# A two-layer decoder trunk in float32: chunk order of the opening, and the last matmuls and root of the end

## The chip, the cores and the metric

The kernel runs on one core of one Trainium2 chip. The time is that of one execution on the device, in microseconds; the median of several runs counts.

## The reference

Two layers over 256 tokens of width 1024, all in float32. Each layer is: x plus half a SwiGLU feed-forward (width 2816) of the normalised x, then x plus a token mixer, then x plus half another SwiGLU. The mixer of layer 0 pools and convolves, that of layer 1 is a gated spatial unit. A last RMSNorm ends it.

```python
def rms_norm(x, g):
    y = x * lax.rsqrt(jnp.mean(x * x, axis=-1, keepdims=True) + EPS)
    return y * g
def swiglu_ffn(x, w_in, w_out):
    gate, up = jnp.split(x @ w_in, 2, axis=-1)
    return (jax.nn.silu(gate) * up) @ w_out
...
for i in range(DEPTH):
    x = x + 0.5 * swiglu_ffn(rms_norm(x, ffn1_norm[i]), ffn1_w_in[i], ffn1_w_out[i])
    x = x + (pool_conv_mixer if i % 2 == 0 else sgu_mixer)(rms_norm(x, mix_norm[i]), ...)
    x = x + 0.5 * swiglu_ffn(rms_norm(x, ffn2_norm[i]), ffn2_w_in[i], ffn2_w_out[i])
return rms_norm(x, final_norm)
```

## The kernel before

The 256 tokens are two tiles of 128 (t = 0, 1). Every float32 operand is kept as a high part (`w_hi`, `xn_hi`, `act_hi`) and a low part (`w_lo`, `xn_lo`, `act_lo`), and `three` makes a product of three matmuls: high x high, high x low, low x high. Weights come in slabs of 128 x 2048 (1 MB), 154 of the feed-forwards and mixers in the order of use. SP loads a slab into one of three `raw` buffers, ScalarE copies it to `w_hi` (ring of six), VectorE subtracts and writes `w_lo` (`lo_split` counts finished slabs). The load of slab n waits until slab n-3 has been split by VectorE. Each engine has its order written out by hand, and semaphores tie them together.

A feed-forward takes units of 256 hidden columns: one slab holds gate and up columns side by side for the first four 128-row chunks of the 1024 inputs, the next slab for the last four. For each token tile the eight chunks accumulate in one bank (`ga` for tile 0, `ub` for tile 1), 512 columns wide. ScalarE takes the Silu of the gate half (`gate_rows`), VectorE multiplies (`product_rows`, which frees the bank) and block-transposes (`to_blocks`); small transfers finish the transpose, and `step_out` multiplies with a slab of `w_out` into four accumulators `acc[t][h]` (token tile t, column half h).

The opening (first unit, slabs 0 and 1, then 2 and 3) is special. The input x arrives in four quarters (`load_x(t, h)`), slabs 0 and 1 in four transfers each (`load_quarters`): a landed pair of chunks counts in `early_landed[n]`, the second pair in `raw_landed[n]`. TensorE transposes x (`first_pairs(t)` the first half of tile t in pairs of chunks, `transposes(0, t, (1,))` the second half), ScalarE writes high parts (`pair_hi`, `second_hi`), VectorE low parts (`pair_lo`, `second_lo`). The norm's root isn't applied to x but later, in `gate_rows` and `product_rows`. `piece` splits part of a slab: `hi_piece` and `lo_piece` count the parts. `opening_unit` runs, by `chunk_rows`, chunks 0 to 3 of tile 0 (with the transposes of tile 1 ahead of chunk 2 and those of tile 0's second half ahead of chunk 3), chunks 0 to 3 of tile 1, then 4 to 7 of tile 0, then 4 to 7 of tile 1. Before it stand warm-up matmuls on constants, some of which wait for the first high parts, low parts and piece.

At the end `slab_out` of the last slab adds both 128-row parts to `acc[1][0]` and `acc[1][1]`, part by part; `half_out` tells VectorE that the left half is complete, `slab_used` the right one. `final(1)` then adds to the residual, multiplies by the last gain, ScalarE squares and sums each half (`ms`), VectorE adds the two sums and EPS (`ms_eps`), GpSimd takes the root (`root`, a power of -0.5), VectorE scales the left half and ScalarE the right half, and SP stores both.

## Time and profile before

| | us |
|---|---|
| median of 3 runs | 893.14 (893.04 to 893.53) |
| the profiled execution | 892.8 |
| its span, first to last instruction | 891.1 |
| TensorE busy in the span | 883.0 (99%) |
| VectorE busy | 566.5 (64%) |
| ScalarE busy | 420.8 (47%) |
| GpSimd busy | 55.6 (6%) |
| mean granted clock of TensorE | 0.998 |

The span leaves out 1.7 us around the instructions. In the page L followed by a number is a line of the kernel, PE is TensorE, PEld its weight loads, DVE VectorE, ACT ScalarE, POOL GpSimd, SP the queue that issues the loads and stores. `w_hi`, `xn_hi` and so on are the program's names for buffers. A busy TensorE includes the time that a matmul spends in the pipeline: a wide matmul (128x512) is shown with 0.39 us.

### The profile page before, as it was taken

How to read it: one execution, taken by the hardware profiler on the slowest of the kernel's cores; microseconds unless marked ns; L12 is line 12 of the kernel's file. 1: busy time of each engine (PE TensorE's matmuls, PEld its weight loads, DVE VectorE, ACT ScalarE, POOL GpSimd, SP SyncE). 2: the span in 40 equal slices, each digit the busy share in tenths (PEclk: the TensorE clock that was granted, in tenths of full speed). 3: DMA queues.
4: the chain of work that ended last, by engine and by line, in shares of the span. 5: the costliest groups of instructions: out<-in, count | busy, mean ns of one | idle time of the engine just before them, and what ended most of it. 6: DMA issues, size and time to landing. Idle time of an engine off the chain costs nothing.

```text
span 891.1 us, 11345 instructions
## 1 busy us (share of the span) xinstructions
PE 883.0 (99%) x4130; PEld 739.0 (83%) x4130; DVE 566.5 (64%) x595; ACT 420.8 (47%) x470; POOL 55.6 (6%) x60
## 2 busy tenths in 40 slices
PE   9999999999999999999999999999999999999997
PEld 8888888889888888888888888888899888888885
DVE  5865565578967756556477556555778666656643
ACT  7644443358744635345345444343663445434432
POOL 1000000406710000000000000000010000000000
PEclk9999999999999999999999999999999999999999
DMA  8987566545254975776639756746575368675721
GB/s 285 294 271 241 178 220 236 177 142 192 70 188 129 300 233 178 243 239 218 208 99 298 258 183 216 240 164 189 168 283 164 120 192 273 216 239 165 240 90 48
DMA packets 149933, 180.18 MB, mean 202 GB/s; under 512 B 7885, under 2 KB 134377, under 8 KB 149896
## 3 DMA queue, kind: packets, MB, share of 16 engines
q1 hardware_dynamic: 149880, 179.67, 61.7%
q8 instruction: 24, 0.39, 0.2%
q14 instruction: 13, 0.11, 0.0%
q10 hardware_dynamic: 16, 0.00, 0.0%
HBM read 168.11 MB, written 1.05 MB: 190 GB/s over the span
## 4 chain that ended last, share of the span: by engine, by line
PE 96%; issue 1%; POOL 1%; ACT 1%; DVE 0%; POOLq 0%; ACTq 0%
PE ga L1246 10%; PE ub L1246 10%; PE ga L1248 10%; PE ub L1248 10%; PE ga L1247 10%; PE ub L1247 10%; PE acc L1246 10%; PE acc L1248 10%; PE acc L1247 10%; PE tp L1308 1%; PE ga L1432 1%; POOL w_lo L509 1%; PE ga L1521 0%; PE tp L1614 0%; DVE w_lo L858 0%
## 5 line engine op out<-in xcount | busy, mean ns | idle before, releaser
L858 DVE TENSOR_TENSOR w_lo<-raw,w_hi 128x2048 fp32r<-128x2048 f32 x147 | 333.4, 2291 | 75.0 <-ACT w_hi L549 73.0
L549 ACT ACTIVATE w_hi<-raw 128x2048 fp32r<-128x2048 f32 x151 | 284.2, 1907 | 21.8 <-DMA raw<-in_ffn_w_in_dram 12.7
L1246 PE MATMUL acc<-w_hi,act_hi 128*128 128x512 f32 x416 | 163.8, 394 | 0.0
L1248 PE MATMUL acc<-w_hi,act_lo 128*128 128x512 f32 x416 | 162.0, 390 | 0.0
L1247 PE MATMUL acc<-w_lo,act_hi 128*128 128x512 f32 x416 | 161.9, 389 | 0.0
L1246 PE MATMUL ga<-w_hi,xn_hi 128*128 128x512 f32 x384 | 150.7, 393 | 0.0
L1246 PE MATMUL ub<-w_hi,xn_hi 128*128 128x512 f32 x384 | 149.5, 389 | 0.0
L1248 PE MATMUL ga<-w_hi,xn_lo 128*128 128x512 f32 x384 | 149.5, 389 | 0.0
L1247 PE MATMUL ga<-w_lo,xn_hi 128*128 128x512 f32 x384 | 149.5, 389 | 0.0
L1248 PE MATMUL ub<-w_hi,xn_lo 128*128 128x512 f32 x384 | 149.5, 389 | 0.0
L1247 PE MATMUL ub<-w_lo,xn_hi 128*128 128x512 f32 x384 | 149.4, 389 | 0.0
L1248 PEld LDWEIGHTS acc<-w_hi,act_lo 128*128 128x128 f32 x416 | 78.1, 188 | 16.5
L1247 PEld LDWEIGHTS acc<-w_lo,act_hi 128*128 128x128 f32 x416 | 78.2, 188 | 15.6
L1246 PEld LDWEIGHTS acc<-w_hi,act_hi 128*128 128x128 f32 x416 | 78.1, 188 | 15.5
L1248 PEld LDWEIGHTS ga<-w_hi,xn_lo 128*128 128x128 f32 x384 | 72.1, 188 | 15.2
L1248 PEld LDWEIGHTS ub<-w_hi,xn_lo 128*128 128x128 f32 x384 | 72.1, 188 | 15.1
L1246 PEld LDWEIGHTS ub<-w_hi,xn_hi 128*128 128x128 f32 x384 | 72.1, 188 | 15.0
L1247 PEld LDWEIGHTS ub<-w_lo,xn_hi 128*128 128x128 f32 x384 | 72.1, 188 | 14.8
L1246 PEld LDWEIGHTS ga<-w_hi,xn_hi 128*128 128x128 f32 x384 | 72.1, 188 | 14.7
L1247 PEld LDWEIGHTS ga<-w_lo,xn_hi 128*128 128x128 f32 x384 | 72.2, 188 | 14.2
L665 ACT ACTIVATE sgh<-ga 128x256 f32<-128x256 f32 x34 | 13.0, 383 | 137.6 <-PE ga L1248 137.4
L1028 DVE TENSOR_TENSOR sgh<-ga,sgh 128x256 f32<-128x256 f32 x34 | 14.4, 423 | 86.7 <-ACT sgh L665 86.7
(160 smaller groups left out, 654.4 us busy)
## 6 DMA issues: line engine op xcount, KB each, us to landing
raw<-in_ffn_w_in_dram SPq DMA_DIRECT2D x172, 512.0 KB, 5.1
raw<-in_ffn_w_out_dram SPq DMA_DIRECT2D x88, 512.0 KB, 4.1
xs<-xs SPq DMA_DIRECT2D x160, 64.0 KB, 2.1
raw<-in_sgu_w_in_dram SPq DMA_DIRECT2D x16, 512.0 KB, 4.8
raw<-in_ab_w_in_dram SPq DMA_DIRECT2D x12, 512.0 KB, 5.1
raw<-in_ab_w_out_dram SPq DMA_DIRECT2D x8, 512.0 KB, 3.8
raw<-in_sgu_w_out_dram SPq DMA_DIRECT2D x8, 512.0 KB, 5.7
raw<-in_ffn_w_in_dram SPq DMA_DIRECT2D x8, 256.0 KB, 5.2
```

The costliest lines, as they stand in the source:

```text
L509: pool.tensor_tensor(w_lo[:, n % RING, :], raw[:, n % RAW, :], w_hi[:, n % RING, :].bitcast(F32), ALU.subtract).then_inc(lo_split, 1)
L549: act.activation(w_hi[:, n % RING, :], raw[:, n % RAW, :], ACT.Copy).then_inc(hi_split, 1)
L665: act.activation(sgh[:, 0, t, :], row[t][:, 0:WIDTH], func).then_inc(gated, 1)
L858: dve.tensor_tensor(w_lo[:, n % RING, :], raw[:, n % RAW, :], w_hi[:, n % RING, :].bitcast(F32), ALU.subtract).then_inc(lo_split, 1)
L1028: dve.tensor_tensor(sgh[:, 1, t, :], row[t][:, WIDTH:WIDE], sgh[:, 0, t, :], ALU.mult)\
L1246: pe.matmul(dst, s_hi, m_hi, start=start, stop=False)
L1247: pe.matmul(dst, s_hi, m_lo, start=False, stop=False)
L1248: return pe.matmul(dst, s_lo, m_hi, start=False, stop=stop)
L1308: mm = pe.transpose(bank[:, c * P:(c + 1) * P], (xs if k else xres)[:, t, o:o + P], ident[:, :])
L1432: pe.matmul(ga[:, 0, 0:P], ones[:, :], avg[:, :], start=True, stop=True)
```

## The change

The four x quarters and the quarters of slabs 0 to 2 are issued in another order and slab 2 comes in quarters too (`load_pair`, third semaphore `early_landed[2]`). In the opening, TensorE takes chunks for both tiles from each pair of chunks that lands (`chunk` in place of `chunk_rows`); ScalarE's and VectorE's order follows it, slab 1 is split in four pieces and slab 3 in two. Eight warm-up matmuls go, with their three waits. At the end, tile 1's last slab is done bank by bank (`last_out`): left half, then columns 512 to 767, then columns 768 to 1023, these into the bank `ga` instead of `acc[1][1]`. VectorE adds each as it is complete (`last_final`), ScalarE squares three parts, GpSimd adds EPS and the three sums in turn and takes the root (`last_root`), and ScalarE and VectorE change halves; VectorE's scaling of the right half takes root and gain in one instruction.

```diff
...
-            def load_quarters(n, w, half, o):
-
-                src = in_view(w)[:, 4 * half:4 * half + 4]
+            def load_pair(n, w, c, a, o, landed):
+
+                src = in_view(w)[:, c:c + 2]
                 slab = raw[:, n, :].rearrange("p (c n) -> p c n", n=WIDE)
-                for a, landed in ((0, early_landed[n]), (2, raw_landed[n])):
-                    for j, c in enumerate(o):
-                        sp.dma_start(slab[:, a:a + 2, j * WIDTH:(j + 1) * WIDTH], src[:, a:a + 2, c])\
-                            .then_inc(landed, 16)
+                for j, cols in enumerate(o):
+                    sp.dma_start(slab[:, a:a + 2, j * WIDTH:(j + 1) * WIDTH], src[:, :, cols]).then_inc(landed, 16)
 
             for k, (kind, w_in, w_out, _) in enumerate(stages):
                 b, d = base[k], ffn0[k] // STEPS * TURNS
                 if kind == "ffn":
                     if k == 0:
                         load_x(0, 0)
-                        load_quarters(0, w_in, 0, pair(0, FF))
+                        load_pair(0, w_in, 0, 0, pair(0, FF), early_landed[0])
                         load_x(1, 0)
+                        load_pair(0, w_in, 2, 2, pair(0, FF), raw_landed[0])
                         load_x(0, 1)
+                        load_pair(1, w_in, 4, 0, pair(0, FF), early_landed[1])
                         load_x(1, 1)
-                        load_quarters(1, w_in, 1, pair(0, FF))
+                        load_pair(1, w_in, 6, 2, pair(0, FF), raw_landed[1])
+                        load_pair(2, w_in, 0, 0, pair(WIDTH, FF), early_landed[2])
+                        load_pair(2, w_in, 2, 2, pair(WIDTH, FF), raw_landed[2])
                     else:
                         load_rows(b, w_in, 0, pair(0, FF))
                         load_rows(b + 1, w_in, 1, pair(0, FF))
-
-                    for a in range(2):
-                        load_rows(b + 2 + a, w_in, a, pair(WIDTH, FF))
+                        load_rows(b + 2, w_in, 0, pair(WIDTH, FF))
+
+                    load_rows(b + 3, w_in, 1, pair(WIDTH, FF))
...
+            def last_root():
+
+                done = 4 * len(stages) + 2
+                pool.memset(eps_tile[:, :], EPS).then_inc(ms_part, 1)
+                pool.wait_ge(ms_part, 1)
+                pool.wait_ge(ms_ready, done + 1)
+                pool.tensor_tensor(ms_sum[:, 0:1], ms[:, 1, 0:1], eps_tile[:, :], ALU.add).then_inc(ms_part, 1)
+                pool.wait_ge(ms_part, 2)
+                pool.wait_ge(ms_ready, done + 2)
+                pool.tensor_tensor(ms_sum[:, 1:2], ms_sum[:, 0:1], ms[:, 1, 1:2], ALU.add).then_inc(ms_part, 1)
+                pool.wait_ge(ms_part, 3)
+                pool.wait_ge(ms_ready, done + 3)
+                pool.tensor_tensor(ms_eps[:, 1:2], ms_sum[:, 1:2], ms_last[:, :], ALU.add).then_inc(ms_part, 1)
+                pool.wait_ge(ms_part, 4)
+                pool.tensor_tensor(rstd[:, 1:2], ms_eps[:, 1:2], minus_half[:, 1:2], ALU.pow)\
+                    .then_inc(rstd_ready, 1)
+
             for k in range(len(stages) + 1):
-                for t in range(TT):
-                    root(t, t + 1)
+                root(0, 1)
+                if k < len(stages):
+                    root(1, 2)
+                else:
+                    last_root()
...
                 piece(0, 0, 512, early_landed[0])
                 pair_hi(0, 1)
                 piece(0, 512, 1024, early_landed[0])
-                piece(0, 1024, 1536, raw_landed[0])
-                piece(0, 1536, 2048, raw_landed[0])
                 square(1, 0)
                 pair_hi(1, 0)
                 pair_hi(1, 1)
+                piece(0, 1024, 1536, raw_landed[0])
+                piece(0, 1536, 2048, raw_landed[0])
+                square(0, 1)
                 second_hi(0)
-                piece(1, 0, 1024, early_landed[1])
-                piece(1, 1024, 2048, raw_landed[1])
+                piece(1, 0, 512, early_landed[1])
+                piece(1, 512, 1024, early_landed[1])
                 second_hi(1)
-                square(0, 1)
-                piece(2, 0, 1024, raw_landed[2])
+                piece(1, 1024, 1536, raw_landed[1])
+                piece(1, 1536, 2048, raw_landed[1])
+                square(1, 1)
+                piece(2, 0, 1024, early_landed[2])
                 gate_rows(0, 0, 0, 0, ACT.Silu, scaled=True)
                 piece(2, 1024, 2048, raw_landed[2])
-                square(1, 1)
-                split(3)
                 gate_rows(1, 0, 0, 0, ACT.Silu, scaled=True)
+                piece(3, 0, 1024, raw_landed[0])
+                piece(3, 1024, 2048, raw_landed[0])
                 nxt = 4
 
             def final(t):
 
                 last = len(stages)
-                for h in range(2):
+                parts = [(0, HALF, ms[:, t, 0:1]), (HALF, D, ms[:, t, 1:2])]
+                if t:
+                    parts[1:] = [(HALF, HALF + T, ms[:, t, 1:2]), (HALF + T, D, ms_last[:, :])]
+                for h, (lo, hi, total) in enumerate(parts):
                     act.wait_ge(x_ready, 4 * (last - 1) + 2 * t + h + 1)
-                    c, o = slice(h * HALF, (h + 1) * HALF), (2 * t + h) * HALF
-                    act.activation(scratch[:, o:o + HALF], xres[:, t, c], ACT.Square, scale=float(D) ** -0.5,
-                                   accum_out=ms[:, t, h:h + 1]).then_inc(ms_ready, 1)
-                act.wait_ge(gained, 2 * t + 2)
+                    act.activation(scratch[:, t * D + lo:t * D + hi], xres[:, t, lo:hi], ACT.Square,
+                                   scale=float(D) ** -0.5, accum_out=total).then_inc(ms_ready, 1)
+                act.wait_ge(gained, (2, 3)[t])
                 act.wait_ge(rstd_ready, ROOTS - 1 + t)
-                act.activation(xs[:, t, HALF:], xs[:, t, HALF:], ACT.Copy, scale=rstd[:, t:t + 1])\
-                    .then_inc(scaled[1], 1)
+                h = 1 - t
+                c = slice(h * HALF, (h + 1) * HALF)
+                act.activation(xs[:, t, c], xs[:, t, c], ACT.Copy, scale=rstd[:, t:t + 1]).then_inc(scaled[h], 1)
...
+            def last_final():
+
+                last, done = len(stages), 4 * (len(stages) - 1) + 2
+                for h in range(2):
+                    dve.wait_ge(half_out, h + 1)
+                    xh = xres[:, 1, h * HALF:(h + 1) * HALF]
+                    dve.scalar_tensor_tensor(out=xh, in0=acc[1][h][:, :], scalar=0.5, in1=xh, op0=ALU.mult,
+                                             op1=ALU.add).then_inc(x_ready, 1)
+                dve.wait_ge(slab_used, base[last])
+                dve.wait_ge(x_ready, done + 2)
+                xh = xres[:, 1, HALF + T:]
+                dve.scalar_tensor_tensor(out=xh, in0=ga[:, 0, :], scalar=0.5, in1=xh, op0=ALU.mult,
+                                         op1=ALU.add).then_inc(x_ready, 1)
+                dve.wait_ge(x_ready, done + 1)
+                dve.tensor_tensor(xs[:, 1, 0:HALF], xres[:, 1, 0:HALF], gain[:, last % 2, 0:HALF], ALU.mult)\
+                    .then_inc(gained, 1)
+                dve.wait_ge(x_ready, done + 3)
+                dve.wait_ge(rstd_ready, ROOTS)
+                dve.scalar_tensor_tensor(out=xs[:, 1, HALF:], in0=xres[:, 1, HALF:], scalar=rstd[:, 1:2],
+                                         in1=gain[:, last % 2, HALF:], op0=ALU.mult, op1=ALU.mult)\
+                    .then_inc(scaled[1], 1)
...
                 piece(0, 0, 512, 1)
                 pair_lo(0, 1)
                 piece(0, 512, 1024, 2)
+                pair_lo(1, 0)
+                pair_lo(1, 1)
                 piece(0, 1024, 1536, 3)
                 piece(0, 1536, 2048, 1)
-                pair_lo(1, 0)
-                pair_lo(1, 1)
                 second_lo(0)
-                piece(1, 0, 1024, 4)
-                piece(1, 1024, 2048, 2)
+                piece(1, 0, 512, 4)
+                piece(1, 512, 1024, 5)
                 second_lo(1)
                 mean_eps(0, 3)
-                piece(2, 0, 1024, 5)
+                piece(1, 1024, 1536, 6)
+                piece(1, 1536, 2048, 2)
+                mean_eps(1, 4)
+                piece(2, 0, 1024, 7)
                 product_rows(0, 0, scaled=True)
                 to_blocks(0, 0)
                 piece(2, 1024, 2048, 3)
-                mean_eps(1, 4)
                 product_rows(1, 0, scaled=True)
                 to_blocks(1, 0)
-                nxt = 3
+                piece(3, 0, 1024, 8)
+                piece(3, 1024, 2048, 4)
+                nxt = 4
...
+            def last_out(n, tile):
+
+                tok = slice(P, 2 * P)
+                for lo, hi in ((0, HALF), (HALF, HALF + T), (HALF + T, D)):
+                    own = hi == D
+                    bank = ga[:, 0, :] if own else acc[1][lo // HALF][:, 0:hi - lo]
+                    for c in range(2):
+                        o = slice(c * D + lo, c * D + hi)
+                        mm = three(bank, act_hi[:, tile + c, tok], act_lo[:, tile + c, tok],
+                                   w_hi[:, n % RING, o], w_lo[:, n % RING, o], own and c == 0, c == 1)
+                    if hi < D:
+                        mm.then_inc(half_out, 1)
                 return mm
 
...
+            def chunk(n, t, c):
 
                 tok = slice(t * P, (t + 1) * P)
+                half, a = c // 4, c % 4
+                if half == 0:
+                    pe.wait_ge(first_lo, 2 * t + a // 2 + 1)
+                elif a == 0:
+                    pe.wait_ge(small_free, small[("norm", 0, t, half)] + 1)
+                if t == 0 and a < 3:
+                    pe.wait_ge(lo_piece, 3 * n + a + 1)
+                elif t == 0:
+                    slab_ready(n)
+                o = slice(a * WIDE, (a + 1) * WIDE)
+                return three(row[t], xn_hi[:, c, tok], xn_lo[:, c, tok], w_hi[:, n, o], w_lo[:, n, o],
+                             c == 0, c == KD - 1)
 
...
-                chunk_rows(0, 0, 0, {2: lambda: first_pairs(1), 3: lambda: transposes(0, 0, (1,))})
-                chunk_rows(0, 1, 0, {3: lambda: transposes(0, 1, (1,))})\
-                    .then_inc(slab_used, 1)
-                chunk_rows(1, 0, 1, {}).then_inc(first_rows, 1)
-                chunk_rows(1, 1, 1, {}).then_inc(slab_used, 1)
+                chunk(0, 0, 0)
+                first_pairs(1)
+                chunk(0, 0, 1)
+                chunk(0, 1, 0)
+                chunk(0, 1, 1)
+                chunk(0, 0, 2)
+                transposes(0, 0, (1,))
+                chunk(0, 0, 3)
+                chunk(0, 1, 2)
+                chunk(0, 1, 3).then_inc(slab_used, 1)
+                transposes(0, 1, (1,))
+                for t in range(TT):
+                    chunk(1, t, 4)
+                    chunk(1, t, 5)
+                chunk(1, 0, 6)
+                chunk(1, 0, 7).then_inc(first_rows, 1)
+                chunk(1, 1, 6)
+                chunk(1, 1, 7).then_inc(slab_used, 1)
 
             def unit(n, f, i=None):
 
-                if n == 2 and i is None:
-                    pe.wait_ge(lo_piece, 5)
+                first = n == 2 and i is None
+                if first:
+                    pe.wait_ge(lo_piece, 7)
                 else:
                     slab_ready(n, i)
                 pe.wait_ge(ga_free, at(f, 2, i))
-                rows_in(n, 0, 0, between={2: lambda: slab_ready(2)} if n == 2 and i is None else None)
+                rows_in(n, 0, 0, between={2: lambda: slab_ready(2)} if first else None)
                 pe.wait_ge(ub_free, at(f, 2, i))
                 rows_in(n, 1, 0).then_inc(slab_used, 1)
-                slab_ready(n + 1, i)
-                rows_in(n + 1, 0, 1).then_inc(first_rows, 1)
+                if first:
+                    pe.wait_ge(lo_piece, 8)
+                else:
+                    slab_ready(n + 1, i)
+                rows_in(n + 1, 0, 1, between={2: lambda: slab_ready(3)} if first else None).then_inc(first_rows, 1)
                 rows_in(n + 1, 1, 1).then_inc(slab_used, 1)
...
             warm_up(WARM_UP)
-            pe.wait_ge(first_hi, 1)
-            warm_up(3)
-            pe.wait_ge(first_lo, 1)
-            warm_up(3)
-            pe.wait_ge(hi_piece, 1)
-            warm_up(2)
...
-                        slab_out(out8 + 2, 1, 4, False, True, half=half_out).then_inc(slab_used, 1)
+                        last_out(out8 + 2, 4).then_inc(slab_used, 1)
...
```

## Rows read from the trace of the kernel before

**Rows 1.** The waits of TensorE in the whole span.

```profile
PE tp L1585 <- POOL rstd L494: 0.5, 1, 0.5
```

**Rows 2.** Timeline of TensorE, 0 to 50 us: start, length, what.

```profile
4.86 3.63 PE L1432 MATMUL ga<-avg,ones 128*128 128x128 f32 x24
8.24 0.48 PE L1246 MATMUL ga<-w_hi,xn_hi 128*128 128x512 f32 x1
...
9.71 0.60 PE L1354 MATMUL acc<-ident,xres 128*128 128x128 f32 x4
...
10.85 0.60 PE L1308 MATMUL tp<-ident,xres 128*128 128x128 f32 x4
...
17.71 0.39 PE L1248 MATMUL ga<-w_hi,xn_lo 128*128 128x512 f32 x1
...
31.54 0.39 PE L1246 MATMUL ga<-w_hi,xn_hi 128*128 128x512 f32 x1
```

**Rows 3.** Timeline of VectorE, 0 to 50 us.

```profile
6.01 0.68 DVE L950 TENSOR_TENSOR w_lo<-raw,w_hi 128x512 fp32r<-128x512 f32 x1
...
10.79 1.13 DVE L956 SCALAR_TENSOR_TENSOR xn_lo<-acc,gain_cols,xn_hi 128x128 fp32r<-128x128 f32 x4 [0.94 <-ACT xn_hi L586]
12.66 1.13 DVE L956 SCALAR_TENSOR_TENSOR xn_lo<-tp,gain_cols,xn_hi 128x128 fp32r<-128x128 f32 x4 [0.74 <-ACT xn_hi L586]
13.70 2.35 DVE L950 TENSOR_TENSOR w_lo<-raw,w_hi 128x1024 fp32r<-128x1024 f32 x2
...
19.74 1.19 DVE L950 TENSOR_TENSOR w_lo<-raw,w_hi 128x1024 fp32r<-128x1024 f32 x1
...
30.64 0.48 DVE L1024 SCALAR_TENSOR_TENSOR sgh<-ga,rstd,sgh 128x256 f32<-128x256 f32 x1
```

**Rows 4.** Timeline of all engines around 250 us.

```profile
249.67 0.71 POOL L494 TENSOR_TENSOR rstd<-ms_eps,minus_half 128x2 f32<-128x2 f32 x1 [2.47 <-DVE ms_eps L1177]
...
250.52 0.35 PE L1585 MATMUL tp<-ident,rstd 128*128 128x128 f32 x1 [0.52 <-POOL rstd L494]
```

**Rows 5.** Transfers issued at 2.25 us: last number, us to landing.

```profile
raw<-in_ffn_w_in_dram SPq DMA_DIRECT2D x1, 256.0 KB, 3.8
```

**Rows 6.** Timeline of SP, 20 to 75 us.

```profile
20.95 0.92 SPq L287 DMA_DIRECT2D raw<-in_ffn_w_in_dram  x2
```

**Rows 7.** Timeline of TensorE, 210 to 211.6 us.

```profile
210.20 0.28 PE L1247 MATMUL ub<-xn_lo,w_hi 128*128 128x256 f32 x1
...
211.40 0.28 PE L1248 MATMUL ub<-xn_hi,w_lo 128*128 128x256 f32 x1
```

**Rows 8.** Timeline of all engines, 884 to 889 us.

```profile
884.11 1.37 DVE L928 SCALAR_TENSOR_TENSOR xres<-acc,xres 128x512 f32<-128x512 f32 x2 [3.73 <-PE acc L1248]
...
884.36 0.39 PE L1248 MATMUL acc<-w_hi,act_lo 128*128 128x512 f32 x1
884.83 0.63 ACT L636 ACTIVATE scratch<-xres 128x512 f32<-128x512 f32 x1 [4.16 <-DVE xres L928]
...
886.88 0.54 POOL L494 TENSOR_TENSOR rstd<-ms_eps,minus_half 128x1 f32<-128x1 f32 x1 [7.02 <-DVE ms_eps L937]
...
887.52 0.72 ACT L640 ACTIVATE xs<-xs,rstd 128x512 f32<-128x512 f32 x1 [1.28 <-POOL rstd L494]
887.97 0.81 SPq L440 DMA_DIRECT2D out_dram<-xs  x2
```

**Rows 9.** Groups of GpSimd by line and shape: busy us, mean ns.

```profile
L519 POOL TENSOR_TENSOR xs<-xs,sgh 128x512 f32<-128x512 f32 x8 | 10.2, 1280 | 4.1 <-ACT sgh L746 3.4
...
L522 POOL TENSOR_TENSOR xs<-xs 128x256 f32<-128x256 f32 x1 | 0.7, 736 | 0.1
```

**Rows 10.** Timeline of GpSimd, 17 to 19 us.

```profile
17.30 0.55 POOL L494 TENSOR_TENSOR rstd<-ms_eps,minus_half 128x1 f32<-128x1 f32 x1 [13.76 <-DVE ms_eps L979]
```

**Rows 11.** Busy time by stretch; after five engines granted clock, DMA share, GB/s.

```profile
884.00:886.00 2.00, 0.75 (x4) 0.28 (x2) 1.89 (x4) 1.17 (x3) 0.00 (x0) 1.00 0.00 0
...
888.00:891.10 3.10, 0.00 (x0) 0.00 (x0) 0.00 (x0) 0.24 (x1) 0.00 (x0) 0.50 0.45 169
```

More of the change, by code:

```diff
@@ L214, in hybrid_trunk @@
         gain_cols_ready = sem("gain_cols_ready")
-        early_landed = [sem(f"early_landed{n}") for n in range(2)]
+        early_landed = [sem(f"early_landed{n}") for n in range(3)]
         gain_landed = [sem(f"gain_landed{i}") for i in range(2)]
@@ L571, in piece @@
             def piece(n, lo, hi, landed):
[L573 to L574 removed]
+                act.wait_ge(landed, 32 * (n // RAW + 1))
+                act.activation(w_hi[:, n, lo:hi], raw[:, n % RAW, lo:hi], ACT.Copy)\
                     .then_inc(hi_split if hi == SLAB else hi_piece, 1)
@@ L1237, in _ @@
                         split_to(b + 11 + 2 * half)
-            for t in range(TT):
-                final(t)
+            final(0)
+            last_final()
         @block.tensor
@@ L1276, in rows_in, with slab_out @@
                 return mm
-            def slab_out(n, t, tile, start, stop, between=None, half=None, parts=(0, 1)):
+            def slab_out(n, t, tile, start, stop, between=None, parts=(0, 1)):
                 tok = slice(t * P, (t + 1) * P)
@@ L1287, in slab_out @@
                                    w_hi[:, n % RING, o], w_lo[:, n % RING, o], start and c == 0, stop and c == 1)
-                        if half is not None and (c, h) == (1, 0):
-                            mm.then_inc(half, 1)
+                return mm
+            def last_out(n, tile):
[9 more added lines that the diff above has]
+                        mm.then_inc(half_out, 1)
                 return mm
@@ L1415, in tail @@
                             ready(a)
-                        between = half = None
+                        between = None
                         if last and t == TT - 1:
-                            if k + 1 < len(stages):
-                                between = lambda h: transposes(k + 1, 0, (h,))
-                            else:
-                                half = half_out
-                        mm = slab_out(n, t, tile, start == n, last, between, half)
+                            between = lambda h: transposes(k + 1, 0, (h,))
+                        mm = slab_out(n, t, tile, start == n, last, between)
                         if t == TT - 1:
```

34 lines of the change are left out of this document (6 added, 28 removed).

## The prediction

> **What bounds the kernel now.** I read the waits of the matmul engine first. Besides the very start, where it waits for the first memset, the view has one row: 0.5 us behind a root of the first mixer [rows 1]. Then its timeline: from 8.24 us, the first matmul of slab 0, to the last one it goes from one matmul to the next [rows 2]. Between 17.71 and 31.54 lie twenty chunks of three matmuls and one more matmul, so a chunk takes 0.68 us; with the restart behind other work the first takes 0.79 (two take 1.47, 8.24 to 9.71) [rows 2]. So the time is the moment of the first real matmul, plus work that never pauses, plus the tail behind the last matmul. Slabs are ready early enough everywhere, but in the opening only just. An edit can win only by an earlier start or a shorter tail, and whatever pause it makes in between is lost, since nothing later waits for anything that could absorb it.
>
> **The start, a gain.** Eight warm-up matmuls go (16 of the 24 records from 4.86 on); those left end before 6.7 us at any pace that fits 24 records in 3.4 us [rows 2]. The first chunk then waits for VectorE's first piece, which ends at 6.01 + 0.68 = 6.69 [rows 3]. What a restart costs, one row shows: GpSimd's root ended at 249.67 + 0.71 = 250.38 and the matmul engine started at 250.52, so 0.14 us [rows 4]. Start: 6.83 instead of 8.24, a gain of 1.41.
>
> **First pause.** The new order is chunk 0 of tile 0, transposes of tile 1, chunk 1 of tile 0, then chunks 0 and 1 of tile 1. The transposes start at 6.83 + 0.79 = 7.62. They need tile 1's first half, now the fourth transfer to be issued; before, the fourth, issued at about 2.2, took 3.8 us [rows 5], so about 6.0, in time. Before, VectorE began the low parts 10.79 - 9.71 = 1.08 after these transposes, and four of them take 1.13, so two take some 0.61 [rows 2, 3]. Low parts ready: 7.62 + 1.08 + 0.61 = 9.31, matmul at 9.45. The engine itself is free at 7.62 + 10.85 - 9.71 = 8.76. Pause 0.69. Before, two chunks and a set of transposes lay between these transposes and tile 1's chunk 0, and covered it.
>
> **Second pause.** Behind the 9.45 come three chunks (0.79, 0.68, 0.68), then the transposes of tile 0's second half at 11.60, where they had begun at 10.85. So a chunk order that starts 1.4 us earlier brings these transposes 0.75 later. From them to the first piece of slab 1 on VectorE it was 13.70 - 10.85 = 2.85 [rows 2, 3], all of it high parts on ScalarE and low parts on VectorE, in series. Now 14.45, the half-size piece takes 0.68, matmul at 15.27. The engine: transposes and one chunk 1.14, two chunks 1.36, and the last transposes (14.10) 0.36, free at 14.46. Pause 0.81. The head start is gone: before, this chunk started four chunks ahead of 17.71 + 0.23, at 15.22.
>
> **Third pause.** Chunks 4 and 5 of tile 0 end at 15.27 + 0.79 + 0.68 = 16.74. Tile 1's need its second low parts: transposes 14.10, then 12.66 - 10.85 = 1.81 and 1.13 [rows 2, 3], so 17.04, matmul at 17.18. Pause 0.44. Before, this transposing stood one chunk earlier and tile 1 four chunks later.
>
> **Fourth pause.** First rows are complete after two chunks of tile 1 and two more of tile 0: last of these matmuls at 17.18 + 0.79 + 3 x 0.68 - 0.23 = 19.78. From that matmul to VectorE's second half of slab 2 it was 19.74 - 17.71 = 2.03 (gate, product, block transpose stand before it) and the piece takes 1.19 [rows 2, 3]: 19.78 + 2.03 + 1.19 = 23.00, matmul 23.14. The engine starts slab 2 at 21.37 and has two chunks without that half, to 22.73. Pause 0.41. Slab 3 then starts at 23.14 + 0.79 + 5 x 0.68 = 27.33.
>
> **Fifth pause.** The semaphore that frees the third raw slab now comes at 23.00 instead of 20.93, and behind it SP queues slab 5. Before: piece done 19.74 + 1.19, issue 20.95 [rows 6]; then the transfer, ScalarE's and VectorE's split, and the first product of slabs 2 and 3 at 30.64, which stands behind slab 5 in VectorE's order and takes 0.48 [rows 3]. Together 30.64 + 0.48 - 20.93 = 10.19 from the semaphore. Now 33.19, matmul 33.33; the engine arrives at 27.33 + 8 x 0.68 = 32.77, so pause 0.56 and 0.11 for the restart. Before it arrived at 31.54, after 31.12 + 0.14: 0.28 of room. Slab 4 comes later too, but it is split ahead of slab 5, which leaves it a whole split of room more. Opening in sum: 33.44 less 31.54, +1.9 us, and no later place gives it back, since the engine waits there for nothing but a chain that it feeds itself.
>
> **Small parts of the opening.** The two transfers of slab 2 become four, two issues more on SP (0.46 each); slab 3 waits for VectorE's last piece of slab 0, now behind tile 1's low parts and so about 1.2 later. Costed at nothing: ScalarE comes to slab 3 behind the second gate, past 21.5, ten microseconds after the issue. Without that cover it would be those 1.2. The square sums on ScalarE only change places.
>
> **The tail.** Six wide matmuls become twelve of 256 columns. Such ones stand in the mixers: ten steps from 210.20 to 211.40, 0.12 each, and last 0.28 where wide ones last 0.39 [rows 7, 8]. Last result: 884.36 - 5 x 0.227 + 11 x 0.12 + 0.28 = 884.83, before 884.75, so +0.08. VectorE's second wide add starts with the sixth narrow matmul's result, 884.11, and takes 0.69 (two take 1.37) [rows 8]; the quarter add of 128x256 from a bank takes 0.48 like the product [rows 3]: 885.37. ScalarE's square of 512 columns takes 0.63 [rows 8] and its sum is then read; for 256 I take 0.5 with that: 885.91. GpSimd adds (below), then its root of 0.54, then 0.10 and 0.72 for ScalarE's scaling, then the store [rows 8]. The add of 128x1 isn't in the trace. GpSimd takes 1.28 us for 512 and 0.74 for 256 columns [rows 9], a straight line that leaves 0.2 for one column; the root, the nearest row in shape, took 0.54, and 0 is the floor. I take 0.2. Root done 886.75 instead of 887.42, first store out at 887.57 instead of 887.97, the second 0.4 behind as before: -0.4. With 0.54 it is -0.06, with nothing -0.6.
>
> VectorE's gain product, two inputs from SBUF, now lies beside the GpSimd add (885.4 to 886.05). In the opening a root ran while VectorE split slab 2, a subtraction of two such inputs, and took 0.55 against 0.54 at the end [rows 8, 10], so I keep 0.4. The Trainium skill (SBUF — State Buffer, Who interferes with whom) says that such a VectorE instruction contends with GpSimd's reads. By it the add would start at 886.05, and the tail gives 0.3 instead of 0.4.
>
> **Sum.** +1.9 - 0.4 = +1.5. The profiled execution took 892.8 (span 891.1), and the median of the runs is 893.14, 0.3 above; so the profile goes to 894.3 and the median to 894.7.
>
> **Rivals.**
> 1. *The head start survives* (the other side): the low parts of tile 1 and of the second halves come as soon as the matmul engine asks. It needs VectorE done by 8.62 instead of 9.31 and by 14.3 instead of 15.13, and no pauses four and five. Then -1.4 - 0.4, 891.3. For it speaks only the start; the distances above, each taken from the same instructions, speak against it. Faster than 892.9 is reached if under 0.2 of pauses are left.
> 2. *No fifth pause*: slab 5's transfer finds the queue emptier and is 0.6 faster. +1.25 - 0.4, 894.0. Its issue comes 2.1 later, so more of slab 4 is out of the way; against it, slab 4's own issue moves along.
> 3. *Tile 1's first half is late*: it is a share of a full queue; each bit that it lands past 7.6 moves all that follows by as much. With half a microsecond: 895.2.
> 4. *The clock drops.* The granted clock is 1.00 up to the end and 0.50 (1.2 instead of 2.4 GHz) in the last stretch, after the engine had stopped at 884.75 [rows 11]. The opening now has a gap of some 0.2 before the first chunk and two of 0.7 to 0.8. If these bring the lower level, each chunk costs 0.68 more; over the four chunks to the second transposes +2.7: 897.4. No pause is as long as the one at the end.
> The Trainium skill (TensorE: Matmul & The Clock Gate, Part 1) has the clock follow the engine's recent activity, which removed warm-ups lower; by it the sum stays as long as the pauses stay short, and rival 4 comes true otherwise.
>
> **Numbers.** Forecast case 0.50 (own range 894.1 to 895.3), rival 1 0.05, rival 2 0.20, rival 3 0.13, rival 4 0.07, other 0.05. Range 893.3 to 896.0: from rival 2 with the longer tail gain and one pause less, to rival 3 with GpSimd's add at 0.54. About 0.2% (1.8 us) can be told from no change. The bound on the slow side is 894.9, just above the forecast: of the forecast case a third lies beyond it, of rival 3 most, rival 4 all. Slower 0.37, within 0.57, faster 0.06.
>
> **What would show it.** First matmul of slab 0 near 6.8; pauses of 0.7, 0.8, 0.4, 0.4 and 0.6 before tile 1's chunk 0, slab 1's chunk 4, tile 1's chunk 4, the second half of slab 2 and slab 4, with VectorE as releaser; the first matmul of slab 4's unit at 33.4; GpSimd's add at 0.2; last store 3.1 behind the last matmul's result. I am wrong if the pauses are shorter because ScalarE or VectorE start sooner behind the transposes than the rows say, or if a later stage has room that I didn't see.

## The result, and the profile after

The changed kernel takes 896.24 us (median of 7 runs, 895.53 to 898.12) against 893.04 us for the kernel before (7 runs, 892.37 to 893.57). The ratio is 1.0039, with a 95% interval of 1.003 to 1.0048: slower by 3.2 us, where 1.5 was forecast. The profiled execution took 897.16 us (span 895.4) and lies 0.9 above its median, so its rows show more loss than the median does.

The waits of TensorE answer to the one row of before [rows 1]; the wait for the first memset at the very start is left out here:

```profile
PE ga L1298 <- DVE sgh L1076: 1.4, 1, 1.4
PE ga L1298 <- DVE w_lo L998: 1.2, 2, 0.7
...
PE tp L1652 <- POOL rstd L500: 0.5, 1, 0.5
PE ub L1298 <- DVE xn_lo L1004: 0.2, 1, 0.2
```

Four waits on VectorE have come, in three rows. One of those on `w_lo` is the start itself (0.65 before slab 0's first matmul); the others are the forecast's second, third and fifth pause. The fourth is so short that the view counts no wait (24.56 in the timeline below), the first isn't there, and the longest is not among the first chunks. The timeline of TensorE over the opening, start and length in front, shows them one by one [rows 2]:

```profile
4.86 1.91 PE L1505 MATMUL ga<-avg,ones 128*128 128x128 f32 x8
7.42 0.76 PE L1298 MATMUL ga<-w_hi,xn_hi 128*128 128x512 f32 x1 [0.65 <-DVE w_lo L998]
7.98 0.63 PE L1299 MATMUL ga<-w_lo,xn_hi 128*128 128x512 f32 x1
8.41 0.63 PE L1300 MATMUL ga<-w_hi,xn_lo 128*128 128x512 f32 x1
8.84 1.05 PE L1413 MATMUL acc<-ident,xres 128*128 128x128 f32 x4
...
10.97 0.45 PE L1298 MATMUL ub<-w_hi,xn_hi 128*128 128x512 f32 x1
...
16.80 0.47 PE L1298 MATMUL ga<-w_hi,xn_hi 128*128 128x512 f32 x1 [0.56 <-DVE w_lo L998]
...
18.63 0.50 PE L1298 MATMUL ub<-w_hi,xn_hi 128*128 128x512 f32 x1 [0.22 <-DVE xn_lo L1004]
...
24.56 0.50 PE L1298 MATMUL ga<-w_hi,xn_hi 128*128 128x512 f32 x1
...
33.99 0.39 PE L1300 MATMUL ub<-w_hi,xn_lo 128*128 128x512 f32 x1
35.77 0.47 PE L1298 MATMUL ga<-w_hi,xn_hi 128*128 128x512 f32 x1 [1.39 <-DVE sgh L1076]
```

Slab 4's unit starts at 35.77 instead of 31.54: 4.23 later, where 1.9 was forecast. The timeline of all engines before it says why the last pause is so long; 0.48 us of VectorE's product releases it:

```profile
30.99 1.92 ACT L575 ACTIVATE w_hi<-raw 128x2048 fp32r<-128x2048 f32 x1 [3.48 <-DMA raw<-in_ffn_w_in_dram]
...
32.81 0.45 ACT L694 ACTIVATE sgh<-ga,rstd 128x256 f32<-128x256 f32 x1
...
32.94 2.29 DVE L890 TENSOR_TENSOR w_lo<-raw,w_hi 128x2048 fp32r<-128x2048 f32 x1 [2.92 <-ACT w_hi L575]
...
35.15 0.48 DVE L1076 SCALAR_TENSOR_TENSOR sgh<-ga,rstd,sgh 128x256 f32<-128x256 f32 x1
```

ScalarE idles for 3.48 us until slab 5's data is there and splits it. Only then does it take the gate of slabs 2 and 3 (32.81), although the bank for it was complete at 31.66. VectorE splits slab 5 too, and only then runs the product (35.15), although its gate was ready at 33.26.

At the end (timeline of all engines), [rows 8] has become:

```profile
888.02 1.40 DVE L976 SCALAR_TENSOR_TENSOR xres<-acc,xres 128x512 f32<-128x512 f32 x2 [3.05 <-PE acc L1300]
...
889.53 0.42 DVE L981 SCALAR_TENSOR_TENSOR xres<-ga,xres 128x256 f32<-128x256 f32 x1
889.61 0.19 POOL L509 TENSOR_TENSOR ms_sum<-ms,eps_tile 128x1 f32<-128x1 f32 x1 [5.12 <-ACT scratch L667]
...
889.87 0.68 DVE L984 TENSOR_TENSOR xs<-xres,gain 128x512 f32<-128x512 f32 x1
...
890.11 0.49 POOL L512 TENSOR_TENSOR ms_sum<-ms_sum,ms 128x1 f32<-128x1 f32 x1 [0.31 <-ACT scratch L667]
890.31 0.19 ACT L667 ACTIVATION_READ_ACCUMULATOR scratch<-xres 128x1 f32 x1
890.68 0.19 POOL L515 TENSOR_TENSOR ms_eps<-ms_sum,ms_last 128x1 f32<-128x1 f32 x1
890.95 0.55 POOL L517 TENSOR_TENSOR rstd<-ms_eps,minus_half 128x1 f32<-128x1 f32 x1
```

The last result is there at 889.13 + 0.28 = 889.41 and the first store starts at 892.33, so 2.92 us; before it was 887.97 - 884.75 = 3.22. One GpSimd add of three takes 0.49 instead of 0.19 us: the one beside VectorE's gain product.

### The profile page after: what moved, and what is told of

Its sections match the earlier page's. It is cut to its first block, busy times and chain, and to the rows that moved or that the text cites. A ratio compares the mean times of both kernels' runs of the same rounds, so it can differ in the third digit from the quotient of the medians.

```text
span 895.4 us, 11339 instructions
## 1 busy us (share of the span) xinstructions
PE 884.7 (99%) x4120; PEld 738.3 (82%) x4120; DVE 567.1 (63%) x597; ACT 421.4 (47%) x475; POOL 57.8 (6%) x64
## 3 DMA queue, kind: packets, MB, share of 16 engines
HBM read 168.11 MB, written 1.05 MB: 189 GB/s over the span
## 4 chain that ended last, share of the span: by engine, by line
PE 95%; ACT 1%; DMA 1%; DVE 1%; POOL 1%; issue 0%; SPq 0%; POOLq 0%; ACTq 0%; DVEq 0%
PE ga L1298 10%; PE acc L1300 10%; PE acc L1298 10%; PE acc L1299 10%; PE ga L1300 10%; PE ub L1298 10%; PE ga L1299 10%; PE ub L1300 10%; PE ub L1299 10%; DMA raw<-in_ffn_w_in_dram 1%; PE tp L1372 1%; POOL w_lo L535 1%; PE ga L1588 0%; PE tp L1681 0%; DVE w_lo L890 0%
```

## The experiments

Each ran against the kernel before on the same chip: 892.97 us (30 runs), 893.01 (33) and 893.22 (21) in the three sets. Three sets of edits come back in several kernels: the warm-ups, the new end, and the order of the product of slabs 2 and 3.

**The change with its eight warm-ups back.**

```
+            pe.wait_ge(first_hi, 1)
+            warm_up(3)
+            pe.wait_ge(first_lo, 1)
+            warm_up(3)
+            pe.wait_ge(hi_piece, 1)
+            warm_up(2)
```

> The changed kernel with the eight warm-up matmuls and their three waits put back; nothing else. If the low pace of the first two chunks (0.43 us between matmuls instead of 0.23) came from the removed warm-ups, matmuls of chunk 0 start at 8.2 to 8.9 us at 0.23 each, and the pause before tile 1's chunk 0 (hidden by the slow chunks in the changed kernel) appears, 0.6 to 0.7 us. The second transposes then start near 13.0 as in the changed kernel (13.12), so the time stays at 2.5 to 3.5 us above the kernel before: removing warm-ups gave nothing. If the order of the chunks is innocent and the warm-ups alone did the harm, the time falls to that of the kernel before less the tail's gain, 892.7. I also expect a smaller spread from run to run than the changed kernel's 2.6 us if that spread comes from where the clock rises.

Measured: 895.99 us (8 runs, 894.96 to 896.85), ratio 1.0031 (1.0021 to 1.0042). Slab 0's first matmul comes at 8.21 as in the kernel before, and yet tile 1's first chunk comes 0.24 us earlier than in the changed kernel:

```profile
9.35 0.48 PE L1298 MATMUL ga<-w_hi,xn_hi 128*128 128x512 f32 x1
...
10.73 0.50 PE L1298 MATMUL ub<-w_hi,xn_hi 128*128 128x512 f32 x1 [0.44 <-DVE xn_lo L1004]
```

With the old start and the new opening the loss is still 3.0 us: the new opening makes it, and the earlier start gave it nothing that the medians show. The pause before slab 4's unit is small here. Slab 5's second transfer took 5.1 us instead of 6.0, and the unit starts 0.59 after TensorE is free:

```profile
34.59 0.47 PE L1298 MATMUL ga<-w_hi,xn_hi 128*128 128x512 f32 x1 [0.42 <-DVE sgh L1076]
```

**The kernel before without the warm-ups** (the same lines removed there).

> The kernel before, less the eight warm-up matmuls and their waits; order of chunks and end as before. Theory clock: the first chunk starts at 6.8 to 7.4 at 0.43 us a matmul, the clock rises at about 10 to 11, and tile 0's chunks take twice as long until then: of the 1.4 us of head start nothing to 0.4 is left, time 892.5 to 893.5. Theory that the head start is worth its size if the order stays: 891.6 to 892.0.

Measured: 893.02 us (11 runs), ratio 1.0001 (0.9992 to 1.001). TensorE starts at 7.07 and is 0.8 us ahead until 30.56. Then all of it goes in one pause, as the timeline of all engines shows:

```profile
27.01 1.92 ACT L549 ACTIVATE w_hi<-raw 128x2048 fp32r<-128x2048 f32 x1 [3.53 <-DMA raw<-in_ffn_w_in_dram]
...
28.96 2.29 DVE L858 TENSOR_TENSOR w_lo<-raw,w_hi 128x2048 fp32r<-128x2048 f32 x1 [1.81 <-ACT w_hi L549]
...
31.17 0.48 DVE L1024 SCALAR_TENSOR_TENSOR sgh<-ga,rstd,sgh 128x256 f32<-128x256 f32 x1
...
31.79 0.47 PE L1246 MATMUL ga<-w_hi,xn_hi 128*128 128x512 f32 x1 [0.84 <-DVE sgh L1024]
```

It is the changed kernel's longest pause in small, in the old order. Slab 5's second transfer took 6.3 us here, against 5.1 in the kernel before. So the place is a limit of its own: the product stands behind a split whose data may be late.

**The kernel before with the new end alone** (`last_out`, `last_root`, `last_final` and the three squares of the change, nothing of its opening).

> The kernel before with the new end alone (last slab bank by bank, three squares, sums and root on GpSimd, swapped halves). Forecast of the prediction: 0.4 us faster, 0.3 if GpSimd's middle add waits beside VectorE's gain product as it did in the changed kernel (0.49 instead of 0.19 us). Rival: the end gives nothing, since the two stores go out 0.4 apart behind the slower ScalarE scaling: 0.0.

Measured: 892.83 us (11 runs), ratio 0.9997 (0.9988 to 1.0006). The end runs within 0.01 us as in the changed kernel: last result 885.18, first store 888.10, again 2.92, and again 0.49 for the middle add. The 0.14 between the medians is in line with the 0.2 that the rows give, and can't be told from nothing by these runs.

**The change with the products ahead of slab 5's split.** On both engines slab 5's split moves behind tile 0's gate or product:

```diff
-                    split_to(b + 5)
+                    split_to(b + (4 if late else 5))
                     for t in range(TT):
                         gate_rows(t, b + 2, r + 1, f + 1, ACT.Silu, scaled=late)
+                        split_to(b + 5)
...
                     for t in range(TT):
                         product_rows(t, g + 2, scaled=late)
+                        split_to(b + 5)
```

> The changed kernel with the first gate and product of slabs 2 and 3 ahead of slab 5's split on ScalarE and VectorE instead of behind it. If the fifth pause (1.55 us before slab 4's unit) is a product queued behind a late slab, as the prediction has it, it vanishes, the unit starts at 34.2 instead of 35.8, and the time falls by 1.5 us to 894.7. If the pause is supply itself (slab 4 or 5 not ready in time), the matmul engine waits at the same place or at slab 5, and the time stays within 0.4 of the changed kernel.

Measured: 893.90 us (11 runs, 893.60 to 894.93), ratio 1.0011 (1.0002 to 1.002). 2.3 us of the 3.2 come back, where 1.5 was expected, and the pause before slab 4's unit is gone: the product runs first, at 31.11, while slab 5 is split on VectorE at 32.85. The profiled execution took 894.76, 0.9 above the median; six of the eleven executions lie between 893.6 and 893.9 and five between 894.5 and 894.9. What parts them is not known.

```profile
31.11 0.49 DVE L1077 SCALAR_TENSOR_TENSOR sgh<-ga,rstd,sgh 128x256 f32<-128x256 f32 x1 [2.25 <-ACT sgh L694]
32.85 2.29 DVE L891 TENSOR_TENSOR w_lo<-raw,w_hi 128x2048 fp32r<-128x2048 f32 x1 [1.25 <-ACT w_hi L575]
```

The profiled execution also started on time, and so it is the clean test of the opening's arithmetic (section on the prediction). TensorE's timeline:

```profile
4.86 1.47 PE L1507 MATMUL ga<-avg,ones 128*128 128x128 f32 x8
6.84 0.47 PE L1300 MATMUL ga<-w_hi,xn_hi 128*128 128x512 f32 x1 [0.53 <-DVE w_lo L999]
7.15 0.40 PE L1301 MATMUL ga<-w_lo,xn_hi 128*128 128x512 f32 x1
7.38 0.40 PE L1302 MATMUL ga<-w_hi,xn_lo 128*128 128x512 f32 x1
7.65 0.66 PE L1415 MATMUL acc<-ident,xres 128*128 128x128 f32 x4
...
9.56 0.50 PE L1300 MATMUL ub<-w_hi,xn_hi 128*128 128x512 f32 x1 [0.56 <-DVE xn_lo L1005]
```

**The kernel before with that order of the products alone.**

> The kernel before with only the order of products and gates of slabs 2 and 3 changed (ahead of slab 5's split). Main theory: the kernel before has no pause of size at slab 4's unit (0.56 us between its last matmul and the unit's first), so at most some tenths come of it: 892.6 to 893.0 us. Rival: the order alone is what gained 2.3 us in the changed kernel, whatever the rest is, and part of it comes here too: below 892.3 us.

Measured: 892.86 us (11 runs), ratio 1.0 (0.9991 to 1.0009). Where nothing is early, the order is worth nothing; the rival falls.

**The kernel before without warm-ups, with that order and the new end.**

> The kernel before without its eight warm-up matmuls, with the products and gates of slabs 2 and 3 put ahead of slab 5's split on VectorE and ScalarE, and with the new end. Main theory: the head start of 0.8 to 1.0 us that the run without warm-ups had until 30.56 us was lost in one pause of 1.23 us before slab 4's unit, because slab 2's product stood on VectorE behind the split of slab 5, whose data came late. With the product ahead of the split the pause goes and the head start of about 0.8 us stays: 893.0 - 0.8 - 0.15 (new end) = about 892.0 us, faster than both kernels. Rival: the head start is limited by the supply of slabs, so that the wait only moves to a later slab: no unit is early any more by 60 us, and the time is 892.8 to 893.0 us.

Measured: 892.04 us (11 runs, 891.63 to 892.82), ratio 0.999 (0.9981 to 0.9999). It beats both kernels, by 1.0 us (the interval ends just below 1) and by 4.2. TensorE's timeline has no pause before slab 4's unit, which starts 0.80 ahead of before [rows 2]:

```profile
30.51 0.39 PE L1293 MATMUL ub<-w_hi,xn_lo 128*128 128x512 f32 x1
30.74 0.39 PE L1291 MATMUL ga<-w_hi,xn_hi 128*128 128x512 f32 x1
```

Each of the three edits alone made no difference that can be measured. Together they do, since the first gives a head start that only the second lets pass. The first two without the new end, which is worth 0.1 to 0.2, were not run.

**The change with the products ahead and the second transposes earlier.** In TensorE's order:

```diff
                 chunk(0, 0, 1)
+                transposes(0, 0, (1,))
                 chunk(0, 1, 0)
                 chunk(0, 1, 1)
                 chunk(0, 0, 2)
-                transposes(0, 0, (1,))
+                transposes(0, 1, (1,))
                 chunk(0, 0, 3)
                 chunk(0, 1, 2)
                 chunk(0, 1, 3).then_inc(slab_used, 1)
-                transposes(0, 1, (1,))
```

> The changed kernel with the products ahead of slab 5's split (893.9 us) and with the second transposes of tile 0 and of tile 1 issued earlier on TensorE: tile 0's directly behind its second chunk, tile 1's before tile 0's fourth chunk. Main theory: the pauses of TensorE in the opening (1.1 us on w_lo in two, 0.8 us on xn_lo in two) are what is left of the loss; work that is put into the first of them shortens the later ones: 893.0 to 893.5 us. Rival: ScalarE's and VectorE's own orders, which are unchanged, bind: the pauses stay, 893.7 to 894.0 us.

Measured: 892.99 us (11 runs, 892.19 to 893.66), ratio 1.0 (0.9991 to 1.0009): 0.9 us less than with the products alone. Past the first memset, the only wait of TensorE that is left in the whole span is the one of before [rows 1]:

```profile
PE tp L1654 <- POOL rstd L500: 0.5, 1, 0.5
```

The transposes fill the first pause, and the pieces that depend on them come before they are asked for. Two tiles per landed piece can thus be fed without a wait, but the result only equals the kernel before. The profiled executions of this kernel and of the one before it in this list differ by only 0.1 in span (890.5 and 890.4), their medians by 0.95; why this one's executions lie higher was not found.

**The change with the earlier transposes alone.**

> The changed kernel (896.2 us) with the earlier transposes alone; products stay behind slab 5's split. Theory of two separate losses: the opening's pauses go as in the run with both edits, so the middle slabs are about 2 us ahead of the changed kernel, and the pause before slab 4's unit grows, since slab 5's data does not come earlier by as much: 1.2 to 2.5 us there, 894.0 to 895.0 us in all. Rival: with the opening in order, slab 5's transfer is as early as in the run with both edits and nothing is queued behind it: no pause, 893.0 us.

Measured: 895.05 us (11 runs, 894.36 to 896.99), ratio 1.0021 (1.0012 to 1.003). The pause before slab 4's unit stays, with 0.96 us between the starts of the two matmuls instead of 0.23:

```profile
32.91 0.39 PE L1300 MATMUL ub<-w_hi,xn_lo 128*128 128x512 f32 x1
33.87 0.47 PE L1298 MATMUL ga<-w_hi,xn_hi 128*128 128x512 f32 x1 [0.57 <-DVE sgh L1076]
```

The pause is shorter than expected, and the median a little above the range given. The four two-tile kernels make a square: 896.2, with earlier transposes 895.05 (-1.2), with earlier products 893.9 (-2.3), with both 893.0 (-3.2). The two edits nearly add up: two losses, each with a place of its own. This profiled execution began late as well: slab 0's first matmul came at 7.82.

**The new end with the gain product behind GpSimd's third add.**

```diff
-                dve.wait_ge(x_ready, done + 1)
+                dve.wait_ge(ms_part, 4)
                 dve.tensor_tensor(xs[:, 1, 0:HALF], xres[:, 1, 0:HALF], gain[:, last % 2, 0:HALF], ALU.mult)
```

> The kernel before with the new end, in which VectorE's two-input product with the gain over the left half of tile 1 waits until GpSimd's third add is done. Main theory: the middle GpSimd add took 0.49 us instead of 0.19 because that product ran beside it; without it the add takes 0.19, and the third add can start as soon as the last square's sum is there, so that the root starts about 0.1 us earlier: first store 0.1 us earlier after the last result, 892.7 us. VectorE's product (0.68 us) then runs beside the root (0.55 us) and ends about 0.2 us after it, so its last multiply with the root may wait for it: that would give back the 0.1. Rival: the add takes 0.49 whatever runs beside it.

Measured: 893.18 us (11 runs), ratio 1.0003 (0.9994 to 1.0012). The middle add takes 0.19, and the root beside the product takes 1.05 instead of 0.55:

```profile
885.67 0.19 POOL L510 TENSOR_TENSOR ms_sum<-ms_sum,ms 128x1 f32<-128x1 f32 x1 [0.31 <-ACT scratch L662]
...
886.42 0.69 DVE L979 TENSOR_TENSOR xs<-xres,gain 128x512 f32<-128x512 f32 x1 [0.91 <-POOL ms_eps L513]
886.46 1.05 POOL L515 TENSOR_TENSOR rstd<-ms_eps,minus_half 128x1 f32<-128x1 f32 x1
```

The delay moves with the product. The first store comes 888.36 - 884.97 = 3.39 after the last result. The expectation had the add right and missed that the root would be hit in turn.

**The new end with a one-input copy instead of the gain product.**

```diff
-                dve.tensor_tensor(xs[:, 1, 0:HALF], xres[:, 1, 0:HALF], gain[:, last % 2, 0:HALF], ALU.mult)
+                dve.tensor_scalar(xs[:, 1, 0:HALF], xres[:, 1, 0:HALF], 1.0, None, ALU.mult)
```

> The kernel before with the new end, in which VectorE's product of the left half of tile 1 with the gain (two inputs from SBUF) is a plain copy times 1.0 (one input from SBUF); this leaves the gain out of that half. Theory: it is the second input of VectorE's product that holds GpSimd's reads, so the middle GpSimd add takes 0.19 us instead of 0.49, the third add starts right behind the last square's sum (0.1 us earlier), and the first store starts 2.8 instead of 2.92 us after the last result's ready time. Rival: any VectorE instruction of 512 elements beside it does so, and the add takes as much longer as the copy still has to run.

Measured: 892.88 us (11 runs), ratio 0.9995 (0.9986 to 1.0004). This kernel leaves the gain out of that half. The add lies beside the copy for 0.18 us and takes 0.22:

```profile
885.37 0.42 DVE L979 TENSOR_SCALAR xs<-xres 128x512 f32<-128x512 f32 x1
...
885.61 0.22 POOL L510 TENSOR_TENSOR ms_sum<-ms_sum,ms 128x1 f32<-128x1 f32 x1 [0.31 <-ACT scratch L662]
```

This run does not tell theory from rival. The add beside the product ended 0.05 us behind the product (890.60 and 890.55 in the changed kernel), and this one ends 0.04 behind the copy (885.83 and 885.79), so a copy that held it as well would look the same. What tells is the first add of the changed kernel: it lies wholly beside VectorE's add of the last quarter (889.53 to 889.95), which has one input in SBUF and one in a bank, and takes 0.19. So not every VectorE instruction delays GpSimd; whether a copy does stays open.

The first store comes 887.79 - 884.91 = 2.88 after the last result, against 2.92, so a third of what was expected: the 0.27 that the add saves lies almost wholly ahead of the last sum, which sets the end.

## Why the prediction was right or wrong

The side was right and so were four of the five pauses; the size was half of what came. Two terms of the sum failed. The start was taken as 6.83 us with matmuls at full pace from there, and the lower clock stood outside the sum, as rival 4: the first matmul came at 7.42 and the lower pace lasted until 11 us. And the 10.19 us from the freed raw slab to the product was carried over as a constant: it was 11.13. In the profiled executions the forecast was +1.5 and the rows show +4.4 (892.8 to 897.16). The 2.9 between them split as follows, in this one execution; between the medians only 1.7 are to be explained.

**The start and the first chunks, +1.4.** The start should have been 6.83 and came at 7.42. ScalarE's second weight piece waited 0.56 us for its transfer and began at 5.92; with products ahead, in the same issue order at the same times, it began at 5.25 and TensorE at 6.84. In the five profiled kernels with this order it began at 5.25, 5.26, 5.39, 5.92 and 6.31: the landing scatters by about 1 us, and the prediction had such a delay only for tile 1's half (rival 3). Then the pace: 0.42 to 0.43 us from one 512-column matmul to the next, instead of 0.23, until 10.97. That is 512 columns at 1.2 GHz, rival 4's lower level. The profile's row for the stretch seems to deny it (1.00, the number after the five engines):

```profile
7.40:11.00 3.60, 3.58 (x11) 2.73 (x12) 1.83 (x7) 2.29 (x8) 0.00 (x0) 1.00 1.07 377
```

But the trace holds no record of the clock there. Its first record, of the full level, begins at 11.04 us, where the pace doubles, and the view prints 1.00 for what has no record. The prediction leaned on the same 1.00: in the kernel before the first record begins at 6.50, in the middle of the warm-ups that it read as one row.

So rival 4, given 0.07, came true in part. It was priced for four chunks, with a gap of some 0.2 ahead of the first; the gap was 0.65 and two chunks were slow. It cost 0.63 on the first chunk. Together with the late start the transposes came 1.22 late (8.84 instead of 7.62); the slow transposes and second chunk then filled the first pause and 0.3 more, so tile 1's chunk came at 10.97 instead of 9.45, 1.5 late. From there to the second half of slab 2 the distances were as forecast: 24.56 - 10.97 = 13.59 against 23.14 - 9.45 = 13.69.

**Pauses one to four, right.** In the run with products ahead, which started on time and at full pace, the forecast marks 6.83, 7.62, 9.45, 15.27, 17.18, 21.37 and 23.14 came at 6.84, 7.65, 9.56, 15.63, 17.47, 21.72 and 23.40. This run is rival 2 made to order, no fifth pause, and its median of 893.9 us meets the 894.0 given for it. The execution whose marks these are took 894.76, though, 0.5 of which it lost at 655 us (below), so in part that meeting is luck. In it and in the run with warm-ups the first pause is seen, 0.72 and 0.60 from where TensorE was free, against 0.69. Tile 1's first half, reckoned for 6.0, landed at 7.61 there, just in time for the transposes at 7.65.

**The fifth pause, mis-sized by 0.9 in this execution.** The distance from the freed raw slab to the end of the product was taken over from before as 10.19 us. It became 35.63 - 24.50 = 11.13, since slab 5's second transfer, issued at 24.9, took 6.0 us to landing instead of 5.1. Rival 2 had hoped for 0.6 less; it was 0.9 more. The pause was 1.55 against 0.67 with the restart. But the distance differs between executions: it was 10.14 in the change with its warm-ups, 10.31 with the transposes alone, and 11.41 in the kernel before without its warm-ups, where the second transfer took 5.1, 5.2 and 6.3 us. So 0.9 is this execution's draw, not a size for the median, and with 10.14 the median was still 895.99.

What the runs add: the place is as weak in the old order. In the run without warm-ups TensorE and the semaphore both came 0.7 earlier, so the 0.28 of room should have stayed; slab 5 landed 0.5 later than before all the same, and the head start was lost. The pause was also fixed by an order, not by work: two lines take it away.

**Later in the span, +0.35.** The prediction said that no later place adds anything. Some 0.1 more is lost by 39 us, and at a step of the second mixer, at 657 us, TensorE takes 0.51 from one matmul to the next (657.43 to 657.94) where before it took 0.23 (653.18 to 653.41). The timeline of ScalarE shows the fifth pause's pattern again: the instruction that frees the bank stands behind the split of a slab whose data is late, and TensorE starts 0.14 after it ends.

```profile
655.40 1.92 ACT L575 ACTIVATE w_hi<-raw 128x2048 fp32r<-128x2048 f32 x1 [3.01 <-DMA raw<-in_sgu_w_in_dram]
657.22 0.58 ACT L861 ACTIVATE xs<-ga 128x512 f32<-128x512 f32 x1
```

Before, that instruction ended at 652.48, 0.93 ahead of the matmul. It comes late by this pattern too in the two-tile kernels with one or both of the later edits and in both kernels on the old order without warm-ups, where TensorE's step takes 0.30 to 0.71. An edit of this place was not run.

**The removed warm-ups.** Their 1.41 came whole at the start of the two kernels that began at 6.84, and 1.17 of it in the two on the old order that began at 7.07. Where the fifth place stayed as it was, it gave nothing that the medians show: 893.02 against 892.97 on the old order, and in the change 896.24 against 895.99 with them put back.

**The end, -0.4 forecast, -0.2 in the rows.** The last result came 0.08 later by the narrow matmuls as reckoned, the last sum 1.09 after it (forecast 1.08), the add took 0.19 (0.2), the root 0.55, and from root to store 0.83 (0.82). Short by 0.16 was the way from the last sum to the end of the root: 891.50 - 890.50 = 1.00 against 0.84. In the kernel with the one-input copy it is 0.94, so 0.06 is VectorE's product and 0.1 are two hand-overs to GpSimd of 0.13 and 0.08 instead of one of 0.1. The row that spoke against the contention was read wrongly: in [rows 10] the root begins at 17.30, and the VectorE piece beside it at 17.41, behind the root's start. The Trainium skill (SBUF — State Buffer, Who interferes with whom) says that a VectorE instruction with two inputs in SBUF contends with GpSimd's reads. The traces agree: 0.49 for 0.19 and 1.05 for 0.55 beside such a product, and no delay beside the add with one input in SBUF and one in a bank. Its sum of 0.3 for the end was the nearer one.

**Chances.** 0.37 stood on slower, and the range ended at 896.0, 0.24 below the median. What it lacked was a case in which two things come late at once, the start and slab 5, though both wait for transfers of the same queue, and a case in which a late start and the lower clock go together. How the 1.7 us between the medians divide over these terms stays open, since one execution of each kernel was profiled.

## What to carry to other kernels

A head start is worth what the tightest later place lets through. Before paying for one, follow it to the first instruction that stands in an engine's order behind work whose data may be late, and put ahead of it whatever feeds the engine that sets the time; here that was two lines, and with them edits that had no measurable effect alone came to 1 us. When an order is changed, work that others wait for (transposes here) belongs into the first gap that the new order opens, not where it stood in the old one. And a small GpSimd step on the last chain wants no VectorE instruction with two inputs in SBUF beside it; moving the instruction moves the delay.

## What the runs showed of the hardware

The level of TensorE's clock at the first real matmuls differed between executions. The 128-column records of the warm-ups stand 0.213 us apart at first and 0.111 later, and the trace's record of the full level begins where that changes:

| profiled kernels | full level from | slab 0's first matmul | TensorE idle before it |
|---|---|---|---|
| six with all warm-ups | 5.28 to 7.13 | 7.66 to 8.54 | none |
| with products ahead | 5.70 | 6.84 | 0.53 |
| the best kernel (before without warm-ups, products ahead, new end) | 5.72 | 7.07 | 0.74 |
| products ahead, transposes earlier | 7.19 | 6.84 | under 0.1 |
| before without warm-ups | 7.77 | 7.07 | 0.30 |
| changed | 11.04 | 7.42 | 0.65 |
| transposes earlier alone | 11.27 | 7.82 | 1.05 |

In the six executions in which the engine stayed busy the rise lies between 5.3 and 7.1 us, always ahead of slab 0. Where the eight warm-ups were gone and the rise had not come when TensorE fell idle, it came at 7.2 and 7.8 after short gaps, and only after 11 us with the two long ones; where it had come, a gap of 0.74 took nothing back. In the kernel with products ahead and transposes earlier it comes within slab 0's first matmuls:

```profile
4.86 1.92 PE L1507 MATMUL ga<-avg,ones 128*128 128x128 f32 x8
6.84 0.63 PE L1300 MATMUL ga<-w_hi,xn_hi 128*128 128x512 f32 x1
7.31 0.40 PE L1301 MATMUL ga<-w_lo,xn_hi 128*128 128x512 f32 x1
7.54 0.40 PE L1302 MATMUL ga<-w_hi,xn_lo 128*128 128x512 f32 x1
```

So removing the warm-ups exposes the first chunks to the lower level, and a late first piece goes with a longer stay there. That is read from six executions; no run held the gap fixed. As the views print 1.00 for stretches without a record, at the very start the distance of the matmuls is what to read.
